# The gap between two groups of on-chip buffers: 64 instead of 448 bytes ahead of the weight buffers

## The reference

```python
h = rms_norm(x, g_pre)
h = (silu(h @ w_gate) * (h @ w_up)) @ w_down    # or a mixer: h @ w_qkv ... @ w_o
x = x + rms_norm(h, g_post)
```

## Time and profile before

| | |
|---|---|
| median of 3 runs | 2139.08 us (2131.37 to 2140.52) |
| the profiled execution | 2141.63 us |
| its span, first to last instruction | 2139.8 us |
| TensorE busy | 2051.3 us, 96% |
| VectorE busy | 1389.2 us, 65% |
| ScalarE busy | 944.5 us, 44% |
| granted TensorE clock, mean | 0.974 of 2.4 GHz |

### The profile page before, as it was taken

One profiled execution on the slowest core, in us unless ns is written; L12 is line 12 of the kernel. 1 busy time (PEld: TensorE's weight loads), 2 busy tenths in 40 slices (PEclk: granted clock), 3 DMA queues, 4 the chain that ended last, 5 costly groups with the idle time before them and its releaser, 6 DMA issues.

```text
span 2139.8 us, 37138 instructions
## 1 busy us (share of the span) xinstructions
PE 2051.3 (96%) x15066; PEld 1908.0 (89%) x15066; DVE 1389.2 (65%) x1853; ACT 944.5 (44%) x1258; POOL 33.0 (2%) x48
## 2 busy tenths in 40 slices
PE   7999999999999999999989989999999996999998
PEld 7879989999889989998988878998899895799997
DVE  6867756666757746765766555776577457565773
ACT  4544434444454434444353253444444343644442
POOL 0000000000000000000000010000000000000000
PEclk9999999999999999999998789999999998999999
DMA  7434554443425554554620133455455543142553
GB/s 291 148 128 177 196 206 169 176 151 145 141 107 196 189 205 156 188 205 164 227 74 1 60 126 130 159 195 207 156 193 185 205 181 128 50 158 109 193 193 115
DMA packets 49788, 341.46 MB, mean 160 GB/s; under 512 B 5776, under 2 KB 6544, under 8 KB 9616
## 3 DMA queue, kind: packets, MB, share of 16 engines
q1 hardware_dynamic: 45216, 321.21, 41.9%
q10 hardware_dynamic: 4464, 18.68, 2.4%
HBM read 338.82 MB, written 1.05 MB: 159 GB/s over the span
## 4 chain that ended last, share of the span: by engine, by line
PE 86%; DVE 9%; ACT 2%; issue 1%; POOL 0%; DMA 0%; DVEq 0%; SPq 0%; POOLq 0%; ACTq 0%
PE pj L229 15%; PE pj L228 15%; PE pj L230 15%; PE acc L234 7%; PE acc L236 7%; PE acc L235 7%; PE pj L234 2%; PE pj L235 2%; PE pj L236 2%; PE pj L567 2%; DVE wlo L304 2%; PE pj L573 1%; PE acc L633 1%; PE acc L646 1%; PE mb L657 1%
## 5 line engine op out<-in xcount | busy, mean ns | idle before, releaser
L304 DVE TENSOR_TENSOR wlo<-raw,whi 128x2048 fp32r<-128x2048 f32 x285 | 653.1, 2291 | 302.5 <-ACT whi L297 301.6
L228 PE MATMUL pj<-xh,whi 128*128 128x256 f32 x2704 | 760.6, 281 | 13.8 <-DVE wlo L314 13.3
L229 PE MATMUL pj<-xl,whi 128*128 128x256 f32 x2704 | 758.8, 281 | 0.0
L297 ACT ACTIVATE whi<-raw 128x2048 fp32r<-128x2048 f32 x299 | 569.9, 1910 | 425.2 <-PE acc L236 198.7
L230 PE MATMUL pj<-xh,wlo 128*128 128x256 f32 x2704 | 756.9, 280 | 0.0
L228 PEld LDWEIGHTS pj<-xh,whi 128*128 128x128 f32 x2704 | 511.1, 189 | 17.0 <-issue 15.8
L229 PEld LDWEIGHTS pj<-xl,whi 128*128 128x128 f32 x2704 | 510.1, 189 | 0.1
L230 PEld LDWEIGHTS pj<-xh,wlo 128*128 128x128 f32 x2704 | 508.8, 188 | 0.0
L234 PE MATMUL acc<-whi,AR 128*128 128x512 f32 x656 | 258.1, 394 | 6.7 <-DVE AR L2029 4.4
L235 PE MATMUL acc<-whi,AR 128*128 128x512 f32 x656 | 257.1, 392 | 0.0
L236 PE MATMUL acc<-wlo,AR 128*128 128x512 f32 x656 | 256.9, 392 | 0.0
(11 more groups left out here) (356 smaller groups left out, 2388.7 us busy)
## 6 DMA issues: line engine op xcount, KB each, us to landing
raw<-in_wstream SPq DMA_DIRECT2D x302, 1024.0 KB, 4.8
F<-in_gains ACTq DMA_DIRECT2D x12, 512.0 KB, 4.7
F<-in_rpb ACTq DMA_DIRECT2D x3, 1024.0 KB, 4.7
F<-in_memtok ACTq DMA_DIRECT2D x2, 1024.0 KB, 4.8
F<-in_memin ACTq DMA_DIRECT2D x2, 1024.0 KB, 6.9
F<-in_small ACTq DMA_DIRECT2D x1, 1536.0 KB, 10.7
F<-in_xin SPq DMA_DIRECT2D x2, 512.0 KB, 6.6
xt<-in_xtok SPq DMA_DIRECT2D x1, 1024.0 KB, 12.2
```

The source lines that it names most:

```text
L228: nc.tensor.matmul(o, wh, k_hi, start=first, stop=False, skip_group_check=True)
L229: nc.tensor.matmul(o, wh, k_lo, start=False, stop=False, skip_group_check=True)
L297: nc.scalar.activation(whi[:, gs, :], raw[:, gs, :], ACT.Copy).then_inc(w_hi, 1)
L304: nc.vector.tensor_tensor(wlo[:, gs, :], raw[:, gs, :], whi[:, gs, :].bitcast(F32), ALU.subtract).then_inc(w_lo, 1)
```

## The change

```diff
--- before.py
+++ after.py
@@ -127,7 +127,7 @@
         xt = sb("xt", [P, 2, D])
         xh = sb("xh", [P, KT, T], F32R)
         xl = sb("xl", [P, KT, T], F32R)
-        sb("space", [P, 112])
+        sb("space", [P, 16])
         raw = sb("raw", [P, 3, CHUNK])
         w_at = nc.sbuf_base
         whi = sb("whi", [P, 3, CHUNK], F32R)
```

## The result

The median of 20 runs of the changed kernel is 2125.22 us (2107.77 to 2134.57), that of 20 runs of the kernel before on the same chip 2139.40 us (2129.02 to 2141.70). The ratio of the two is 0.9935, with a 95% interval of 0.9916 to 0.9954: the change makes the kernel 0.65% faster, 14 us. The forecast was 30 us off, 2109. The sign is right and the size is not: less than half came.

A forecast was written before the change was run, and what follows sets the result against it. TensorE's pace from matmul to matmul was taken as the bound; feed-forwards 21.3, slices 2.8, other `tile_fm` matmuls 6.0, minus 0.1 for weights moving, gave 30.0 us off: 2111.6 profiled, 2109 as median, range 2099 to 2147.

The forecast's parts named there:

- The bound, and that nothing but TensorE's pace moves: Whole kernel: TensorE, busy 96% of the span, sets the time; `AR` and output products stay unchanged, supply not late.
- Only the distance matters, not the role: Matmul streams: moving-minus-standing distance modulo 512 sets the pace; the rival that the role decides shared no effect's 0.30, 2139 us.
- The rule that the prediction cites: TensorE reads: moving and standing operands use independent ports, so placement is free and time stays 2139; within no effect's 0.30.
- Slower, at 283: Rival, weights standing: moving stream runs into the standing one, median duration 283 ns, 21.8 us more, 2161 us; chance 0.18.
- Feed-forwards, 21.3 us: Six feed-forwards, 5760 matmuls: 113.3 instead of 117.8 ns, one of six staying slow; gain 21.3 us, ends 0 and 25.6.
- each stage in the pace of its first start: Feed-forwards: every stage keeps the pace, 113.3 or 117.8 ns, that TensorE falls into when the stage first starts.
- 5 in 6: Weights-moving stretches at distance -64 said to begin after a stop: 5 of 6 settle at 113.3 ns; applied to feed-forwards.
- Slices and mixers, 8.8 us: `slices_pe` and the `tile_fm` matmuls outside the feed-forwards: gains of 2.8 us and 6 us at the faster pace.
- the walk: Stages in order with swapped pace rules: 228 other `tile_fm` matmuls left at 117.8, some 1650 gain; weights moving 285 slow.
- The range of 2099 to 2147: Whole kernel, us: holds the forecast and no effect (0.30) with their scatter, leaves out slower (0.18).
- the forecast's own range, 2100 to 2124: Whole kernel, us: low end everything gained, 37 us; high end three more feed-forwards slow, 12.8 us; 2 us scatter each.
- two read streams meet and one waits: TensorE's moving and next standing operand streams now and then meet; one waits 16 columns, making steps 16 to 32 cycles longer.

The follow-up runs named there:

- streams: Bench without the computation: TensorE alone runs 48-matmul streams (21 at 512 columns), each after a stop, at varied operand distances, either operand role; 1088.71 us.
- gap320: The kernel before with a spacer of 320 bytes, distance -320, between activations and weights; 2123.40 us, ratio 0.9924 against the kernel before.
- The bench: Computation left out: two streams at the changed kernel's distance with broadcast products or other matmuls between them; two runs, 1106.91 and 1140.72 us.
- third: The changed kernel with a third broadcast product ahead of the six feed-forwards, without a stop; 2104.34 us, ratio 0.9852 against the kernel before.
- gap0: The kernel before without the spacer, distance 0 between activations and weights; 2162.35 us, ratio 1.0117 against the kernel before.
- gap128: The kernel before with a spacer of 128 bytes, distance -128; 2148.57 us, ratio 1.0060 against the kernel before.
- gap256: The kernel before with a spacer of 256 bytes; 2155.44 us, ratio 1.0109 against the kernel before.
- hand-over benches: Three runs without the computation: streams with different products or stops between or ahead of them, at distances -64 and +64; 1106.91, 1140.72 and 1097.35 us.
- stop: The changed kernel with a wait for VectorE's broadcast copy ahead of the chunks in each of six feed-forwards; 2114.71 us, ratio 0.9897 against the kernel before.

## Why the prediction was partly right

- **The bound, and that nothing but TensorE's pace moves.** Right. `AR` stays at 120.0 and the output products at 226.7 ns per step, the supply is not late, the busy counts are unchanged.
- **Only the distance matters, not the role.** Right (`streams`, both roles alike). The rule that the prediction cites from the Trainium skill, TensorE: Matmul & The Clock Gate, Part 2 (two independent read ports, so that placement would be free), does not describe these rows: one shape, started the same way, goes at 272.0 to 288.0 cycles by the placement. The period is 256 bytes, not 512; for this change it makes no difference.
- **Slower, at 283.** Did not come; the distance -64 never showed 120.0 ns.
- **Feed-forwards, 21.3 us: this is the step that failed.** The text took "each stage in the pace of its first start" and gave that start the share of 5 in 6. The share was pooled over six stretches said to begin after a stop; none did, and only one of them, behind slow slices, followed the broadcast. The pace depends on what runs ahead. In the changed kernel the stretches with the weights standing behind the second attention's L657 are at 113.3 in 6 of 6, as in the rows that the share came from; behind the two broadcast products 8 of 10 are at 117.8, and five of the six feed-forwards are among them. The term measured 4.3 us in place of 21.3 in the profile. With a stop put in, which makes the forecast's premise true, five of six were fast; with the third product six of six.
- **How far that goes.** In the changed kernel and in gap320 together 12 of 12 feed-forwards had the pace opposite to their slices', and 10 of 12 were slow. The bench reproduces the ten at 117.8, behind slices at 113.3. It does not reproduce the two at 113.3, behind slices at 117.8, since in it two products leave a stream at 117.8 where it was: why they were fast is open, as is why the slices are mostly fast.
- **Slices and mixers, 8.8 us.** Over-sized too, and the walk did not come as drawn: it had 1650 + 640 = 2290 matmuls becoming faster, and 2541 - 960 = 1581 did, 7.0 us by count. In the stretches of nine or more outside the feed-forwards 702 matmuls of `tile_fm` were still at 117.8, not 228, and 396 with the weights moving, not 285, which loses 0.5 us. In time it is nearer to half of 8.8. Up to the first feed-forward it is 1.0 us (starts 160.5 and 159.5), but 0.5 of that lies ahead of the first product (13.27 and 12.76); from the first to the second, with the second attention between, 1.4 us (364.8 to 363.4). The further stages can't be read from these two profiles, since their clock differs; gap320, which has the same share of the low clock there as before (61 us), took 411.1 us from the third to the fourth where before took 412.2. In `third`, 28.3 us faster than the line in the clock by the median, six fast feed-forwards (25.6, if all were fast in each execution) and six products (-1.3) leave 4.0 us for slices and mixers. The prediction allowed 1.3 us of the gain to be lost behind the attentions' waits; whether more was, no run here took apart.
- **Scatter.** The spread of the changed kernel is 27 us against 13 before. Six feed-forwards at 4.27 us are 25.6 us, and at equal clock its executions spread over 24 us. Kernels whose feed-forwards all had one pace in the profile, gap0, gap128 and gap256, spread over 3 to 4 us at equal clock (4, 10 and 4 executions). That speaks for a number of slow feed-forwards that differs from run to run. It is not shown directly: only one execution of each kernel has a trace.

The range of 2099 to 2147 holds the result, but it did so for want of a known size: the forecast's own range, 2100 to 2124, misses the median by 1 us. The rival that should have stood there is "the feed-forwards start behind the broadcast, not behind what the 5 in 6 were counted on", with a price of 17 us (four more of them slow).

## What to carry to other kernels

Where a tuned kernel is bound by TensorE, read the step between the starts of matmuls, not their durations or busy shares; one shape has more than one pace. Try the offset between moving and standing buffers (here 192 modulo 256 bytes for float32r with 256 columns, 0 for 512 columns), it costs nothing. Then see what stands ahead of each long stream without a stop: one small product more or less can decide 4% of its time, and one look at a single execution does not tell how often. A share counted over past stretches holds only for stretches with the same thing ahead of them, so look at the line before each one. And compare executions at equal granted clock: the scatter that is left is then the kernel's own.

## What the runs showed of the hardware that was not expected

- The step of a float32r matmul depends on the distance between its operands with a period of 256 bytes: 272.0 (192), 282.7 (64), 285.0 (128) and 288.0 (0) cycles for 256 columns. For 512 columns the best and the worst change places (544 at 0, 560 at 192). I can't explain the numbers. That two read streams meet and one waits is an argument from the prediction that would give multiples of 16 cycles at 256 columns, and the runs neither show it nor exclude it.
- TensorE keeps a pace over more than 900 matmuls, until the stream changes. Two or four float32 broadcast products of 128 columns in front leave a stream at 117.8 ns at the distance -64, one or three leave it at 113.3, in 10 cases of 10 each. It is no rule of odd and even for all products: a single one of 256 columns, or a single float32r one of 128, leaves it at 117.8, 10 of 10 each.
- A stop brings 113.3 back at -64 in most cases: 303 of 336 first streams of the hand-over benches, 31 of 32 in `streams`, five of six feed-forwards of `stop`; but only 4 of 10 behind twelve matmuls of the other role. Why the exceptions are exceptions is open.
